# The opening of a two-block transformer kernel, reordered: weights of blocks 0 and 1 two chunks at a time, block 2 in halves, x on ScalarE's queue, first sum of squares behind block 5

## The chip, the cores and the metric

The kernel runs on one core of a Trainium2 chip. The metric is the device time of one execution in microseconds (us), the median of several runs. The profile is one execution recorded by the hardware profiler on the same kernel; its times are counted from the start of its span.

## What is computed

The reference is a stack of two transformer blocks on x of 256 tokens by 1024 features, all in float32:

```python
x = first_block(x, ...)    # ffn, mixer (indexed attention and pooling), ffn
return second_block(x, ...)  # ffn, gated mixer, ffn, final norm
...
x = x + 0.5 * swiglu(rms_norm(x, ffn1_norm[l]), ffn1_w_gate[l], ffn1_w_up[l], ffn1_w_down[l])
...
def rms_norm(x, g):
    xf = x.astype(jnp.float32)
    y = xf * lax.rsqrt(jnp.mean(xf * xf, axis=-1, keepdims=True) + NORM_EPS)
    return (y * g.astype(jnp.float32)).astype(x.dtype)
def swiglu(x, w_gate, w_up, w_down):
    return (jax.nn.silu(x @ w_gate) * (x @ w_up)) @ w_down
```

The change touches only the start of the first feed-forward stage (`ffn1`), with D = 1024 and 2816 hidden features.

## The kernel before

All weights of the program lie in HBM as one stream of blocks of 128 x 1024 floats (512 KB). A block of the gate or up matrix holds the weights of 128 hidden features for all eight chunks (k = 0 to 7) of 128 input features. Gate and up blocks alternate: block 2f is the gate and 2f + 1 the up of hidden chunk f. The stream passes through a ring of four slots (`RING`): SyncE (SP) issues the DMA of block n as soon as the low part of block n - 4 is made (semaphore `w_split`), ScalarE copies it to `w_hi`, rounded to the short float format of TensorE (`split`, L479), VectorE subtracts to get the remainder `w_lo` (`split`, L867), and TensorE multiplies. x is treated alike: `x_hi` on ScalarE (L486, times the norm's gain), `x_lo` on VectorE (L873), side by side in `x_hl`. TensorE makes two matmuls for each chunk of a block (`both`, L1396 and L1397): high weights times high and low x, 512 columns, then low weights times high x, 256 columns. Eight such pairs make a block (`wide_block`).

The norm is taken out of the matmul: the products are made with x unnormalised, and each result is scaled by `rstd`. Its chain in the first stage is: ScalarE squares the eight chunks of x (`square`, L482), POOL adds them up one after the other (`add_squares`, L382), TensorE sums over the partitions with a matmul by ones (`sum_squares`, L1464), VectorE makes the mean `ms` (L901), ScalarE the root (L520, which has a table load ahead of it), VectorE a reciprocal and three Newton steps (L894 to L897). Only then can VectorE scale the first hidden chunk (`add`: L936 adds the two halves of the products, L938 scales; `product`, L945). POOL issues the DMAs of the constants (L397 to L400) behind its adds.

Each engine runs its own program strictly in the order it is written by hand; the semaphores only make it wait. In `ffn` VectorE makes the low parts of blocks 3 to 6, then `mean_square`, then block 7, then `inverse_root`, then `add(0)`, block 8, `product(0)`, `add(1)`, block 9 and so on. ScalarE makes the high parts of blocks 3 to 7 and then the root.

The opening is written apart. SP loads blocks 0 and 1 in halves of 512 columns (chunks 0 to 3, then 4 to 7), then chunks 4 to 7 of x, then blocks 2 and 3 whole. ScalarE issues x chunks 0 and 1, the column gains `cols`, and x chunks 2 and 3. x comes in four pairs of chunks (`x_loaded`). TensorE first runs `WARM` = 16 matmuls on zeros. It then takes, for each chunk k of x, block 0 and block 1 (`for k ...: for c in range(2)`) into two banks, then blocks 2 and 3, the sum of squares, and blocks 4 and on. Block 7 needs bank 3, in which the sum of squares lies, and waits for `ms_done`:

```python
for f in range(2, LEAD):
    if f == 3:
        pe.wait_ge(ms_done, p + 1)
    elif f >= 4:
        pe.wait_ge(parts_added, FC * e + f - 3)
    chunk(f, (f + 2) % 4)
```

Of the kernel before, what the change touches and what calls it, by code (L numbers as in the profile page):

```python
# [26 lines left out]
P = 128  # L27
# [19 lines left out]
RING = 4  # L47
# [46 lines left out]
def build(nc, stream, x_in, cols_in, rows_in, const_in, sgu_w_in, pool_w_in, gain_in, out):  # L94
    ctx = ExitStack()
    with ctx:
# [110 lines left out]
        half_arrived = [sem(f"half_arrived{i}") for i in range(2)]  # L207
# [136 lines left out]
        def _(sp):  # L344
            for n in range(2):
                sp.dma_start(w_raw[:, n, 0:HALF], stream[n, :, 0:HALF]).then_inc(half_arrived[n], 16)
            for n in range(2):
                sp.dma_start(w_raw[:, n, HALF:BW], stream[n, :, HALF:BW]).then_inc(arrived[n], 16)
            for c in range(2, 4):
                sp.dma_start(x[:, 2 * c:2 * c + 2, :], x_in[:, 2 * c:2 * c + 2, :]).then_inc(x_loaded[c], 16)  # L350
            for n in range(2, RING):
                sp.dma_start(w_raw[:, n, :], stream[n]).then_inc(arrived[n], 16)
# [116 lines left out]
        def _(act):  # L469
# [18 lines left out]
            def first_input():  # L488

                for c in range(4):  # L490
# [3 lines left out]
                    if c == 1:  # L494
                        for n in range(2):
                            act.wait_ge(arrived[n], 16)
                            nc.scalar.activation(w_hi[:, n, HALF:BW], w_raw[:, n, HALF:BW], ACT.Copy).then_inc(w_hi_done, 1)
                    if 1 <= c < 3:
                        square(0, 2 * c - 2)
                        square(0, 2 * c - 1)  # L500
                split(2)
                for k in range(4, KC):
                    square(0, k)
# [18 lines left out]
            def ffn(e, n0, p):  # L522
                for b in range(3, 8):
# [307 lines left out]
            act.dma_start(x[:, 0:2, :], x_in[:, 0:2, :]).then_inc(x_loaded[0], 16)  # L831
            act.dma_start(cols[:, 0:NCOLS], cols_in).then_inc(cols_loaded, 16)
            act.dma_start(x[:, 2:4, :], x_in[:, 2:4, :]).then_inc(x_loaded[1], 16)
            act.wait_ge(filled, 1)
            nc.scalar.activation(spare[:], zeros[:, 0:1], ACT.Copy).then_inc(spare_set, 1)
            for n in range(2):
                act.wait_ge(half_arrived[n], 16)
                nc.scalar.activation(w_hi[:, n, 0:HALF], w_raw[:, n, 0:HALF], ACT.Copy).then_inc(half_hi_done, 1)
            act.wait_ge(cols_loaded, 16)
# [11 lines left out]
        def _(dve):  # L851
# [513 lines left out]
            for n in range(2):  # L1365
# [3 lines left out]
            for k in range(4):  # L1369
                input_lo(0, k)  # L1370
            for n in range(2):
# [3 lines left out]
            for k in range(4, KC):  # L1375
                input_lo(0, k)
            split(2)
# [9 lines left out]
        def _(pe):  # L1387
# [121 lines left out]
            def ffn(e, n0, p):  # L1509

                if p == 0:
                    pe.wait_ge(half_split, 2)
                for k in range(KC):
                    if k == (KC // 2 if p == 0 else 0):
                        pe.wait_ge(w_split, n0 + 2)
                    pe.wait_ge(x_split, 8 * p + k + 1)
                    w = slice(k * P, (k + 1) * P)
                    for c in range(2):
                        slot = (n0 + c) % RING
                        last = both(bank[4 + c][:, :], w_hi[:, slot, w], w_lo[:, slot, w], x_hl[:, k, :, :], k == 0, k == KC - 1)  # L1520
                        if k == KC - 1:
                            last.then_inc(w_used, 1)
                wide_block(n0 + 2, bank[6], x_hl)
# [279 lines left out]
WARM = 16  # L1803
# [112 lines left out]
```

## Time and profile before

| | |
|---|---|
| median of 3 runs | 1060.01 us (1059.9 to 1060.06) |
| the profiled execution's own time | 1060.34 us |
| its span | 1058.5 us |
| mean granted clock of TensorE | 0.999 |
| TensorE busy | 1048.3 us (99%) |
| VectorE busy | 773.9 us (73%) |
| ScalarE busy | 614.1 us (58%) |
| POOL busy | 193.0 us (18%) |
| moved by DMA | 200.53 MB, 189 GB/s on the mean |

The profile gives, for each engine, its instructions in order of time, each with its start, its length, and the idle time before it with the engine or transfer that ended it. ScalarE is called ACT there, VectorE DVE, TensorE PE, its weight loads PEld, and the queue part of an engine has a q (SPq, ACTq). The span is shorter than the execution's own time, which has some 1.8 us around it. The chain of work that ended last is 97% TensorE.

### The profile page before, as it was taken

To read this page: it belongs to the slowest core of one execution; us is meant where nothing else is said; L and a number is where in the kernel's file an instruction comes from. 1 tells how busy PE (TensorE), PEld (TensorE's weight loads), DVE (VectorE), ACT (ScalarE), POOL (GpSimd) and SP (SyncE) were. 2 spreads that over 40 slices of the span, in tenths; PEclk is the share of its full clock that TensorE was granted. 3 is DMA by queue.
4 is the path that set the end of the run, shared out by engine and by line. 5 is a ranking of instruction groups with operands and counts; after the bars stand their busy time and mean duration, and the time that the engine had idled before them with its cause. 6 is when DMAs were issued, how large, how long until landed. Compare 5 with 4: busy or idle time off the path is not lost.

```text
span 1058.5 us, 17547 instructions
## 1 busy us (share of the span) xinstructions
PE 1048.3 (99%) x6112; PEld 920.2 (87%) x6112; DVE 773.9 (73%) x1107; ACT 614.1 (58%) x936; POOL 193.0 (18%) x208
## 2 busy tenths in 40 slices
PE   8999999999999999999999999999999999999997
PEld 6888888888888888888888888889988888888886
DVE  6876776799797666668767666788877778877543
ACT  7655545466765654447565445755655556655542
POOL 4211131020221111101111100133201032311100
PEclk9999999999999999999999999999999999999999
DMA  7855555554266565566555564656555555655552
GB/s 276 290 192 198 190 188 183 175 180 161 98 210 207 190 190 186 191 196 200 198 189 191 180 206 151 224 182 193 176 195 182 185 179 192 224 196 197 176 188 75
DMA packets 55570, 200.53 MB, mean 189 GB/s; under 512 B 6304, under 2 KB 6304, under 8 KB 55392
## 3 DMA queue, kind: packets, MB, share of 16 engines
q1 hardware_dynamic: 54288, 195.85, 56.0%
q0 software_dynamic: 656, 3.18, 0.8%
q10 hardware_dynamic: 576, 0.83, 0.3%
q8 instruction: 32, 0.52, 0.2%
q14 instruction: 18, 0.15, 0.0%
HBM read 198.78 MB, written 1.05 MB: 189 GB/s over the span
## 4 chain that ended last, share of the span: by engine, by line
PE 97%; ACT 1%; DMA 1%; DVE 1%; issue 0%; ACTq 0%; DVEq 0%
PE pair L1396 52%; PE pair L1397 26%; PE pair L1390 6%; PE pair L1391 5%; PE pair L1392 5%; DMA x<-x_in 1%; PE pair L1743 0%; PE pair L1676 0%; PE pair L1663 0%; PE pair L1607 0%; PE pair L1654 0%; PE pair L1464 0%; ACT qk_a L698 0%; ACT x_hl L486 0%; DVE qk_a L1178 0%; PE pair L1640 0%
## 5 line engine op out<-in xcount | busy, mean ns | idle before, releaser
L867 DVE TENSOR_TENSOR w_lo<-w_raw,w_hi 128x1024 fp32r<-128x1024 f32 x369 | 461.6, 1255 | 213.5 <-ACT w_hi L479 212.8
L1396 PE MATMUL pair<-x_hl,w_hi 128*128 128x512 f32 x1728 | 591.5, 390 | 2.6 <-DVE x_hl L873 2.4
L479 ACT ACTIVATE w_hi<-w_raw 128x1024 fp32r<-128x1024 f32 x369 | 386.1, 1057 | 229.9 <-PE pair L1397 181.4
L1397 PE MATMUL pair<-x_hl,w_lo 128*128 128x256 f32 x1728 | 477.8, 277 | 0.0
L1396 PEld LDWEIGHTS pair<-x_hl,w_hi 128*128 128x128 f32 x1728 | 324.4, 188 | 71.0 <-issue 3.2
L1397 PEld LDWEIGHTS pair<-x_hl,w_lo 128*128 128x128 f32 x1728 | 324.3, 188 | 0.1
L1396 PE MATMUL pair<-wide,w_hi 128*128 128x512 f32 x720 | 247.2, 391 | 0.0
L1397 PE MATMUL pair<-wide,w_lo 128*128 128x256 f32 x720 | 199.6, 277 | 0.0
L1396 PEld LDWEIGHTS pair<-wide,w_hi 128*128 128x128 f32 x720 | 135.2, 188 | 28.8
L390 POOL TENSOR_TENSOR wide<-side,wide 128x256 fp32r<-128x256 f32 x88 | 86.6, 984 | 377.4 <-ACT wide L537 377.4
L1397 PEld LDWEIGHTS pair<-wide,w_lo 128*128 128x128 f32 x720 | 135.1, 188 | 0.0
L382 POOL TENSOR_TENSOR x_sq<-x_sq 128x256 f32<-128x256 f32 x42 | 40.4, 962 | 239.3 <-ACT x_sq L482 238.0
L486 ACT ACTIVATE x_hl<-x,cols 128x256 fp32r<-128x256 f32 x48 | 23.5, 507 | 78.0 <-DVE x L984 70.9
L936 DVE TENSOR_TENSOR tmp<-pair,side 128x512 f32<-128x512 f32 x88 | 60.3, 685 | 3.2 <-ACT side L529 2.8
L529 ACT ACTIVATE side<-pair 128x512 f32<-128x512 f32 x88 | 51.0, 580 | 5.2 <-PE pair L1397 5.2
L533 ACT ACTIVATE tmp<-tmp 128x256 f32<-128x256 f32 x88 | 35.9, 408 | 19.5 <-DVE tmp L938 19.5
L938 DVE TENSOR_TENSOR tmp<-tmp,rstd 128x256 f32<-128x256 f32 x88 | 44.2, 502 | 3.1
L1390 PE MATMUL pair<-w_hi,x_hl 128*128 128x512 f32 (+1 forms) x112 | 43.4, 387 | 0.0
L1391 PE MATMUL pair<-w_lo,x_hl 128*128 128x512 f32 (+1 forms) x112 | 42.4, 379 | 0.0
L1392 PE MATMUL pair<-w_hi,x_hl 128*128 128x512 f32 (+1 forms) x112 | 42.4, 379 | 0.0
L537 ACT ACTIVATE wide<-side 128x256 f32 (+1 forms) x88 | 35.9, 408 | 5.2 <-DVE side L945 5.2
L945 DVE TENSOR_TENSOR side<-tmp 128x256 f32<-128x256 f32 x88 | 36.8, 418 | 1.9 <-ACT tmp L533 1.9
(199 smaller groups left out, 860.5 us busy)
## 6 DMA issues: line engine op xcount, KB each, us to landing
w_raw<-stream SPq DMA_DIRECT2D x369, 512.0 KB, 3.3
const<-const_in POOLq DMA_DIRECT2D x1, 1248.0 KB, 8.3
w_raw<-stream SPq DMA_DIRECT2D x4, 256.0 KB, 5.6
rows<-rows_in POOLq DMA_DIRECT2D x1, 576.0 KB, 10.2
x<-x_in ACTq DMA_DIRECT2D x2, 256.0 KB, 5.6
x<-x_in SPq DMA_DIRECT2D x2, 256.0 KB, 6.6
sgu_w<-sgu_w_in POOLq DMA_DIRECT2D x1, 512.0 KB, 12.9
qk_a<-gain_in POOLq DMA_DIRECT2D x1, 512.0 KB, 4.0
```

The source lines that it names most:

```text
L382: nc.gpsimd.tensor_tensor(x_sq[:, 0, :], x_sq[:, 0, :], x_sq[:, k, :], ALU.add).then_inc(x_sq_added, 1)
L390: nc.gpsimd.tensor_tensor(hid_lo[:, f, :], hid_b[:, f % 2, :], hid_hi[:, f, :].bitcast(F32), ALU.subtract).then_inc(hid_split, 1)
L479: nc.scalar.activation(w_hi[:, slot, at:at + BW], w_raw[:, slot, :], ACT.Copy).then_inc(w_hi_done, 1)
L529: nc.scalar.activation(low_s[:], pair[j][:, :, S:2 * S], ACT.Copy).then_inc(low_copied, 1)
L867: nc.vector.tensor_tensor(w_lo[:, slot, :], w_raw[:, slot, :], w_hi[:, slot, at:at + BW].bitcast(F32), ALU.subtract).then_inc(w_split, 1)
L936: nc.vector.tensor_tensor(sum_s, pair[j][:, :, 0:S], low_s[:], ALU.add).then_inc(parts_added, 1)
L938: nc.vector.tensor_tensor(gate_s, gate_s, rstd[:], ALU.mult).then_inc(gate_scaled, 1)
L1390: nc.tensor.matmul(dst, a_hi, b_hi, start=first, stop=False, skip_group_check=True)
L1391: nc.tensor.matmul(dst, a_hi, b_lo, start=False, stop=False, skip_group_check=True)
L1392: return nc.tensor.matmul(dst, a_lo, b_hi, start=False, stop=last, skip_group_check=True)
L1396: nc.tensor.matmul(dst, a_hi, b_hl.rearrange("p a s -> p (a s)"), start=first, stop=False, skip_group_check=True)
L1397: return nc.tensor.matmul(dst[:, 0:S], a_lo, b_hl[:, 0, :], start=False, stop=last, skip_group_check=True)
```

## The change

SP issues the halves of blocks 0 and 1, then block 2 in halves, then block 3 whole; it issues no x any more. ScalarE issues `cols` first and then the four pairs of x. ScalarE and VectorE make their parts in the order half of block 0, pair 0 of x, half of block 1, pair 1, second half of block 0, pair 2, second half of block 1, pair 3, the halves of block 2. On ScalarE all squares but two come behind block 3. TensorE takes two chunks of block 0, the same two chunks of block 1, and so on, and then block 2, waiting for its halves. In the first stage the sum of squares stands behind block 5 instead of block 3, and the wait for `ms_done` stands between blocks 6 and 7. There are 15 matmuls on zeros instead of 16. The other stages keep their order.

```diff
@@ SP @@
-            for n in range(2):
+            def first_half(n):
                 sp.dma_start(w_raw[:, n, 0:HALF], stream[n, :, 0:HALF]).then_inc(half_arrived[n], 16)
-            for n in range(2):
+
+            def second_half(n):
                 sp.dma_start(w_raw[:, n, HALF:BW], stream[n, :, HALF:BW]).then_inc(arrived[n], 16)
-            for c in range(2, 4):
-                sp.dma_start(x[:, 2 * c:2 * c + 2, :], x_in[:, 2 * c:2 * c + 2, :]).then_inc(x_loaded[c], 16)
-            for n in range(2, RING):
-                sp.dma_start(w_raw[:, n, :], stream[n]).then_inc(arrived[n], 16)
+
+            first_half(0)
+            first_half(1)
+            second_half(0)
+            second_half(1)
+            first_half(2)
+            second_half(2)
+            sp.dma_start(w_raw[:, 3, :], stream[3]).then_inc(arrived[3], 16)
@@ ScalarE @@
+                first_half(0)
+                act.wait_ge(cols_loaded, 16)
+                x_pair(0)
+                first_half(1)
+                x_pair(1)
+                second_half(0)
+                x_pair(2)
+                second_half(1)
+                x_pair(3)
+                first_half(2)
+                second_half(2)
+                square(0, 0)
+                square(0, 1)
+                split(3)
+                for k in range(2, KC):
                     square(0, k)
...
-                for b in range(3, 8):
+                for b in range(4 if p == 0 else 3, 8):
                     split(n0 + b)
...
-            act.dma_start(x[:, 0:2, :], x_in[:, 0:2, :]).then_inc(x_loaded[0], 16)
             act.dma_start(cols[:, 0:NCOLS], cols_in).then_inc(cols_loaded, 16)
-            act.dma_start(x[:, 2:4, :], x_in[:, 2:4, :]).then_inc(x_loaded[1], 16)
+            for c in range(4):
+                act.dma_start(x[:, 2 * c:2 * c + 2, :], x_in[:, 2 * c:2 * c + 2, :]).then_inc(x_loaded[c], 16)
@@ VectorE @@
+            first_half(0)
+            input_lo(0, 0)
+            input_lo(0, 1)
+            first_half(1)
+            input_lo(0, 2)
+            input_lo(0, 3)
+            second_half(0)
+            input_lo(0, 4)
+            input_lo(0, 5)
+            second_half(1)
+            input_lo(0, 6)
+            input_lo(0, 7)
+            first_half(2)
+            second_half(2)
             ffn(0, START[0], 0)
@@ TensorE, ffn @@
+                def opening(k, c):
+                    slot, w = (n0 + c) % RING, slice(k * P, (k + 1) * P)
+                    if c == 0:
+                        pe.wait_ge(x_split, 8 * p + k + 1)
+                    last = both(bank[4 + c][:, :], w_hi[:, slot, w], w_lo[:, slot, w], x_hl[:, k, :, :], k == 0, k == KC - 1)
+                    if k == KC - 1:
+                        last.then_inc(w_used, 1)
+
                 if p == 0:
-                    pe.wait_ge(half_split, 2)
...
+                    for two in range(0, KC, 2):
+                        for c in range(2):
+                            if two < KC // 2:
+                                pe.wait_ge(half_split, c + 1)
+                            else:
+                                pe.wait_ge(w_split, c + 1)
+                            opening(two, c)
+                            opening(two + 1, c)
+                    pe.wait_ge(half_split, 3)
+                    for k in range(KC):
+                        if k == KC // 2:
+                            pe.wait_ge(w_split, 3)
+                        opening(k, 2)
...
                 wide_block(n0 + 3, bank[7], x_hl)
-                sum_squares(p)
+                if p:
+                    sum_squares(p)
 
                 def chunk(f, j, i=0):
 
                     wide_block(n0 + 2 * f, bank[2 * j], x_hl, i, 8)
+                    if p == 0 and f == 3:
+                        pe.wait_ge(ms_done, p + 1)
                     wide_block(n0 + 2 * f + 1, bank[2 * j + 1], x_hl, i, 8)
 
                 for f in range(2, LEAD):
-                    if f == 3:
+                    if f == 3 and p == 0:
+                        sum_squares(p)
+                    elif f == 3:
                         pe.wait_ge(ms_done, p + 1)
...
-WARM = 16
+WARM = 15
```

ScalarE's program before, from its first DMA to the high part of block 3 (L486 is a high part of x, L838 and L497 halves of blocks 0 and 1, L482 squares):

```order
L831 DMA x<-x_in 128x512
L832 DMA cols<-cols_in 128x84
L833 DMA x<-x_in 128x512
...
L838 ACTIVATE w_hi<-w_raw 128x512 [waits half_arrived0]
L838 ACTIVATE w_hi<-w_raw 128x512 [waits half_arrived1]
L486 ACTIVATE x_hl<-x,cols 128x256 [waits x_loaded0,cols_loaded]
...
L482 ACTIVATE x_sq<-x 128x256 x4
L479 ACTIVATE w_hi<-w_raw 128x1024 [waits arrived3]
L479 ACTIVATE w_hi<-w_raw 128x1024 [waits w_used,arrived0]
```

The same place in the changed program:

```order
L851 DMA cols<-cols_in 128x84
L853 DMA x<-x_in 128x512 x4
...
L497 ACTIVATE w_hi<-w_raw 128x512 [waits half_arrived0]
L491 ACTIVATE x_hl<-x,cols 128x256 [waits x_loaded0,cols_loaded]
L491 ACTIVATE x_hl<-x,cols 128x256
L497 ACTIVATE w_hi<-w_raw 128x512 [waits half_arrived1]
...
L487 ACTIVATE x_sq<-x 128x256 x2
L484 ACTIVATE w_hi<-w_raw 128x1024 [waits arrived3]
L487 ACTIVATE x_sq<-x 128x256 x6
L484 ACTIVATE w_hi<-w_raw 128x1024 [waits w_used,arrived0]
```

Pair 0 of x has moved ahead of the half of block 1 and behind the gains in the queue, and six squares now stand between blocks 3 and 4.

TensorE around the sum of squares before (pair0 to pair3 are the bank pairs; each block is 16 rows of matmuls, the rows of its other chunks are left out):

```order
L1397 MATMUL pair3<-x_hl,w_lo 128x256
L1464 MATMUL pair1<-x_sq,ones 128x256 [waits x_sq_added]
L1396 MATMUL pair0<-x_hl,w_hi 128x512 [waits w_split]
...
L1396 MATMUL pair1<-x_hl,w_hi 128x512 [waits w_split,ms_done]
```

and in the changed program:

```order
L1424 MATMUL pair0<-x_hl,w_lo 128x256
L1491 MATMUL pair1<-x_sq,ones 128x256 [waits x_sq_added]
L1423 MATMUL pair1<-x_hl,w_hi 128x512 [waits w_split]
...
L1423 MATMUL pair1<-x_hl,w_hi 128x512 [waits w_split,ms_done]
```

The matmul by ones has moved from ahead of block 4 (pair0) to ahead of block 6 (pair1), and the wait for the mean from block 6 to block 7. VectorE's program behind it has kept its order, which reads in the changed program (L883 is a block's low part, L952 and L954 the addition and scaling of a hidden chunk):

```order
L883 TENSOR_TENSOR w_lo<-w_raw,w_hi 128x1024 [waits w_hi_done] x4
L917 TENSOR_SCALAR ms<-pair 128x256 [waits sumsq_done]
L883 TENSOR_TENSOR w_lo<-w_raw,w_hi 128x1024 [waits w_hi_done]
L910 RECIPROCAL rstd<-root 128x256 [waits root_done]
...
L952 TENSOR_TENSOR tmp<-pair,side 128x512 [waits low_copied,rstd_done]
L954 TENSOR_TENSOR tmp<-tmp,rstd 128x256 [waits parts_added]
L883 TENSOR_TENSOR w_lo<-w_raw,w_hi 128x1024 [waits w_hi_done]
```

Of this, only the count ahead of `ms` differs (x4, block 2 having its own halves; before x5).

## Rows read from the trace of the kernel before

**Rows 1.** The page, part 1: busy time, share of the span, instructions

```profile
PE 1048.3 (99%) x6112; PEld 920.2 (87%) x6112; DVE 773.9 (73%) x1107; ACT 614.1 (58%) x936; POOL 193.0 (18%) x208
```

**Rows 2.** Timeline of PE, 0 to 46 us: start, length, engine, line, operation, idle before

```profile
1.33 5.19 PE L1788 MATMUL pair<-zeros 128*128 128x512 bf16 x16 [1.33 <-POOL zeros L372]
8.16 0.47 PE L1396 MATMUL pair<-x_hl,w_hi 128*128 128x512 f32 x1 [1.64 <-DVE x_hl L873]
...
11.97 0.47 PE L1396 MATMUL pair<-x_hl,w_hi 128*128 128x512 f32 x1 [0.78 <-DVE x_hl L873]
...
15.22 0.50 PE L1396 MATMUL pair<-x_hl,w_hi 128*128 128x512 f32 x1 [0.22 <-DVE w_lo L867]
...
20.93 0.59 PE L1464 MATMUL pair<-x_sq,ones 128*128 128x256 f32 x2
...
21.70 0.39 PE L1396 MATMUL pair<-x_hl,w_hi 128*128 128x512 f32 x1
...
24.43 0.39 PE L1396 MATMUL pair<-x_hl,w_hi 128*128 128x512 f32 x1
```

**Rows 3.** Timeline of DVE, 0 to 60 us

```profile
6.07 0.69 DVE L1367 TENSOR_TENSOR w_lo<-w_raw,w_hi 128x512 fp32r<-128x512 f32 x1 [6.07 <-ACT w_hi L838]
...
7.53 0.88 DVE L873 SCALAR_TENSOR_TENSOR x_hl<-x,cols,x_hl 128x256 fp32r<-128x256 f32 x2
...
16.11 6.12 DVE L867 TENSOR_TENSOR w_lo<-w_raw,w_hi 128x1024 fp32r<-128x1024 f32 x4 [0.95 <-ACT w_hi L479]
22.16 0.41 DVE L901 TENSOR_SCALAR ms<-pair 128x256 f32<-128x256 f32 x1
22.49 1.21 DVE L867 TENSOR_TENSOR w_lo<-w_raw,w_hi 128x1024 fp32r<-128x1024 f32 x1
24.01 1.75 DVE L894 RECIPROCAL rstd<-root 128x256 f32<-128x256 f32 x1 [0.31 <-ACT root L520]
...
28.24 1.22 DVE L867 TENSOR_TENSOR w_lo<-w_raw,w_hi 128x1024 fp32r<-128x1024 f32 x1
...
31.28 1.21 DVE L867 TENSOR_TENSOR w_lo<-w_raw,w_hi 128x1024 fp32r<-128x1024 f32 x1
...
34.31 1.21 DVE L867 TENSOR_TENSOR w_lo<-w_raw,w_hi 128x1024 fp32r<-128x1024 f32 x1
```

**Rows 4.** Timeline of ACT, 0 to 60 us

```profile
5.40 0.63 ACT L838 ACTIVATE w_hi<-w_raw 128x512 fp32r<-128x512 f32 x1 [1.74 <-DMA w_raw<-stream]
6.26 0.63 ACT L838 ACTIVATE w_hi<-w_raw 128x512 fp32r<-128x512 f32 x1 [0.22 <-DMA w_raw<-stream]
6.79 0.89 ACT L486 ACTIVATE x_hl<-x,cols 128x256 fp32r<-128x256 f32 x2
8.17 0.91 ACT L486 ACTIVATE x_hl<-x,cols 128x256 fp32r<-128x256 f32 x2 [0.48 <-DMA x<-x_in]
...
13.80 1.33 ACT L482 ACTIVATE x_sq<-x 128x256 f32<-128x256 f32 x4
15.03 2.95 ACT L479 ACTIVATE w_hi<-w_raw 128x1024 fp32r<-128x1024 f32 x3
...
22.27 1.28 ACT L520 ACT_TABLE_LOAD   x1
23.56 0.42 ACT L520 ACTIVATE root<-ms 128x256 f32<-128x256 f32 x1
```

**Rows 5.** SP's issues of x (timeline), and the time to landing at line L350

```profile
2.61 1.43 SPq L350 DMA_DIRECT2D x<-x_in  x2
...
DMA to landing us min/median/max: 6.6/6.6/6.6
```

**Rows 6.** Timeline of POOL, 0 to 60 us

```profile
14.29 5.73 POOL L382 TENSOR_TENSOR x_sq<-x_sq 128x256 f32<-128x256 f32 x4 [0.59 <-ACT x_sq L482]
```

**Rows 7.** The same sum of squares in the last feed-forward stage, timeline 880.5 to 882 us

```profile
881.00 0.59 PE L1464 MATMUL pair<-x_sq,ones 128*128 128x256 f32 x2
...
881.63 0.42 DVE L901 TENSOR_SCALAR ms<-pair 128x256 f32<-128x256 f32 x1 [0.85 <-PE pair L1464]
```

More of the change, by code:

```diff
@@ L206, in build @@
         arrived = [sem(f"arrived{i}") for i in range(RING)]
-        half_arrived = [sem(f"half_arrived{i}") for i in range(2)]
+        half_arrived = [sem(f"half_arrived{i}") for i in range(3)]
         half_hi_done = sem("half_hi_done")
@@ L488, in first_input, with first_half, second_half, x_pair @@
             def first_input():
-                for c in range(4):
+                def first_half(n):
+                    act.wait_ge(half_arrived[n], 16)
+                    nc.scalar.activation(w_hi[:, n, 0:HALF], w_raw[:, n, 0:HALF], ACT.Copy).then_inc(half_hi_done, 1)
+                def second_half(n):
+                    act.wait_ge(arrived[n], 16)
+                    nc.scalar.activation(w_hi[:, n, HALF:BW], w_raw[:, n, HALF:BW], ACT.Copy).then_inc(w_hi_done, 1)
+                def x_pair(c):
                     act.wait_ge(x_loaded[c], 16)
@@ L493, in first_input @@
                     input_hi(0, 2 * c + 1)
[L494 to L502, printed above, removed]
+                first_half(0)
[13 more added lines that the diff above has]
+                for k in range(2, KC):
                     square(0, k)
@@ L829, in gated_mixer @@
                     square(p + 1, m)
-            act.dma_start(x[:, 0:2, :], x_in[:, 0:2, :]).then_inc(x_loaded[0], 16)
             act.dma_start(cols[:, 0:NCOLS], cols_in).then_inc(cols_loaded, 16)
-            act.dma_start(x[:, 2:4, :], x_in[:, 2:4, :]).then_inc(x_loaded[1], 16)
+            for c in range(4):
+                act.dma_start(x[:, 2 * c:2 * c + 2, :], x_in[:, 2 * c:2 * c + 2, :]).then_inc(x_loaded[c], 16)
             act.wait_ge(filled, 1)
             nc.scalar.activation(spare[:], zeros[:, 0:1], ACT.Copy).then_inc(spare_set, 1)
[L836 to L839, printed above, removed]
             first_input()
@@ L1363, in gated_mixer, with first_half @@
                 input_lo(p + 1, KC - 1)
-            for n in range(2):
+            def first_half(n):
                 dve.wait_ge(half_hi_done, n + 1)
@@ L1368, in _, with second_half @@
                                         ALU.subtract).then_inc(half_split, 1)
-            for k in range(4):
-                input_lo(0, k)
-            for n in range(2):
+            def second_half(n):
                 dve.wait_ge(w_hi_done, n + 1)
@@ L1374, in _ @@
                                         ALU.subtract).then_inc(w_split, 1)
-            for k in range(4, KC):
-                input_lo(0, k)
-            split(2)
+            first_half(0)
[12 more added lines that the diff above has]
+            second_half(2)
             ffn(0, START[0], 0)
@@ L1509, in ffn @@
             def ffn(e, n0, p):
-                if p == 0:
-                    pe.wait_ge(half_split, 2)
[L1513 to L1522, printed above, removed]
@@ L1523, in ffn @@
-                wide_block(n0 + 2, bank[6], x_hl)
+                def opening(k, c):
[5 more added lines that the diff above has]
+                        last.then_inc(w_used, 1)
+                if p == 0:
+                    for two in range(0, KC, 2):
[11 more added lines that the diff above has]
+                        opening(k, 2)
+                else:
+                    pe.wait_ge(w_split, n0 + 2)
+                    for k in range(KC):
+                        for c in range(2):
+                            opening(k, c)
+                    wide_block(n0 + 2, bank[6], x_hl)
```

## The prediction, made before the changed kernel was run

> **What bounds the kernel now.** I began with the busy time of the page: TensorE is busy for 1048.3 of 1058.5 us [rows 1], so only some 10 us of the span can be won without giving TensorE less to do, and the change gives it one warm matmul less and nothing else. Next I read TensorE's own timeline for where these 10 us lie. From 1.33 to 6.52 it runs 16 matmuls on zeros; the first real one starts at 8.16; it stops before 11.97 and before 15.22, both times with an idle time written at the row [rows 2]. From there on the pairs of matmuls (512 columns, then 256) follow each other every 0.34 to 0.35 us: two rows that are eight pairs apart stand at 21.70 and 24.43, so that a block costs 2.73 us [rows 2]. I found no TensorE wait between this and the end of the kernel. So the opening is the only stretch from which the change can take time, and everywhere behind it the question is by how much each producer leads TensorE. For that I read the timelines of ScalarE (high parts of weights and x, squares), VectorE (low parts) and POOL (adding squares).
>
> **The opening.** Its ends before: a low half of a block costs VectorE 0.69 us, from 6.07 to 6.76, and two low parts of x take 0.88 us from 7.53 on, the first of them until about 8.0; TensorE starts at 8.16, some 0.15 us later [rows 3, 2]. ScalarE needs 0.53 us from one weight half to the next operation (6.26 to 6.79), 0.40 for a high part of x (0.89 for a pair with the tail of the last), 0.33 for a square and about 0.98 for a whole block [rows 4]. It got pair 1 of x at 8.14 to 8.17, after 0.48 us of waiting for the transfer [rows 4].
>
> With the new order I take ScalarE through its queue. Half of block 0 ends at 6.04, as now (VectorE's row at 6.07 waited for it). Pair 0 of x can then start if it is there; the column gains now go ahead of it on the same queue, so I take its landing at 6.3, which is an estimate: the bytes before it (half of blocks 0 and 1, pair 0, gains) are those that had landed when ScalarE began pair 0 at 6.79 [rows 4]. Then: pair 0 6.3, half of block 1 7.1, pair 1 8.15 (it still waits for its transfer), second half of block 0 8.95, pair 2 9.5, second half of block 1 10.3, pair 3 10.8, block 2 in halves 11.6 and 12.1, squares 0 and 1 12.7, block 3 13.3, the other six squares 14.2, block 4 16.1, block 5 17.1. For pairs 2 and 3 I need landings by 9.5 and 10.8. On the SP queue they were issued from 2.61 on and landed 6.6 us after issue, at 9.2 and 9.9 [rows 5]; now block halves are interleaved with them, and by their place in the sum of the bytes they land at about 9.2 and 10.5, just before they are wanted.
>
> A rule is weighed here: the rows give no sign that a transfer on the other queue would be faster (pair 1, issued by ScalarE, took until 8.14 while the halves were coming on SP). The Trainium skill, page "DMA: Bandwidth & Descriptors", section "Issuing engines are not separate DMA queues", says that transfers from all issuing engines run on the same 16 DMA engines and interleave, and that only issue time is saved. By it my landings stand; were the queues independent, pair 1 could start at 7.65 and TensorE could gain up to 0.5 us more.
>
> VectorE follows ScalarE closely: low half of block 0 6.76, low parts 0 and 1 of x 7.35 and 7.75, half of block 1 8.5, parts 2 and 3 9.2 and 9.6, second half of block 0 10.3, parts 4 and 5 10.7 and 11.1, second half of block 1 11.7, parts 6 and 7 12.1 and 12.5, block 2 13.1 and 13.7. TensorE, 0.35 us a pair of matmuls: 7.5 (two chunks of block 0), 8.65 (block 1), 9.35 to 10.75 (chunks 2 and 3), 10.85 and 11.85 (4 and 5), 12.55 to 13.95 (6 and 7). Block 2 starts at 13.95 and has no wait left, instead of 15.22. **Term one: -1.3 us.** Bounds: 0 if x lands late; at best TensorE starts at 7.5 and never stops, 16 x 0.35 = 5.6 us, block 2 at 13.1, so -2.1.
>
> Edits that cost nothing: the five DMA issues of ScalarE take about 0.45 us each and end near 3.0, the table load of 1.28 us and the spare operation then end near 4.6, before the first half arrives at 5.40 [rows 4] (ScalarE waited for it for 1.74 us; if that cover of 0.8 us went, the opening would move by the rest). One warm matmul fewer ends that stretch about 0.2 us sooner; TensorE stood idle from 6.52 to 8.16 before without a lower granted clock, so a gap from 6.3 to 7.5 is harmless. Block 2 in two halves costs each engine a tenth of a microsecond of start-up, inside the times above.
>
> Blocks 3 and 4 come later on ScalarE, because squares 2 to 7 stand between them: block 4 ends at 17.15 there. VectorE's four blocks from 16.11 took 6.12 us, 1.53 each, beside POOL's adds, whereas one beside nothing took 1.21 [rows 3]. I take 1.7 for block 4: ready at 18.9, wanted at 13.95 + 5.6 = 19.55. It holds, by 0.6 us. The Trainium skill, page "SBUF — State Buffer", section "Who interferes with whom", has VectorE operations with two SBUF inputs and GpSimd take one port pair by turns, each blocked for the whole of the other's instruction. By the mean of the rows (1.53) block 4 has 0.8 us to spare, by a full add of 1.43 us (5.73/4) in its way it would miss by 0.25, and the sum would be that much higher.
>
> **The sum of squares.** POOL's adds took 5.73 us for four [rows 6], 1.43 each; six of them from 15.0 end at 23.6. TensorE reaches the place behind block 5 at T = 13.95 + 16 x 0.35 + 2 x 2.73 = 25.0. So the matmul itself does not wait, and its own 0.43 us is only moved.
>
> What hangs on it does matter. Before, it started at 20.93 and block 6 followed two blocks later. The chain was: ms on VectorE, block 7's low part, root on ScalarE, reciprocal 24.01, three steps, the first block's addition and scaling, then the low part of **block 8** 28.24 to 29.46, blocks 9 and 10 from 31.28 and 34.31 (1.21 each, to 32.49 and 35.52) [rows 3]. In that order VectorE can't touch block 8 before the reciprocal and its Newton steps are through. TensorE wanted block 8 at 21.36 + 4 x 2.73 = 32.3 (21.36 is a pair before the row at 21.70), blocks 9 and 10 at 35.0 and 37.7: leads of 2.8, 2.5 and 2.2 us. The change takes two blocks, 5.46 us, out of that lead. What the chain gets back: ms came 1.23 us after the matmul because VectorE was busy with block 6 [rows 2, 3]; in the last feed-forward stage it came after 0.63 [rows 7], so 0.6. The root's table load of 1.28 us ran until 23.55 [rows 4] and was behind block 7's high part; now both are long done, so the reciprocal starts when block 7's low part ends, 0.63 + 0.33 + 1.24 = 2.2 us after T instead of 3.08. That is 0.88 in all. From the reciprocal on the durations are the same ones, VectorE being busy without a gap.
>
> So block 8 is ready at T + 7.65 and wanted at T + 0.43 + 5.46 = T + 5.9; block 9 at T + 10.7 against T + 8.6; block 10 at T + 13.7 against T + 11.35; block 11 is 1.5 us later than 10 and no longer late. The total of the stall is the largest lateness, 2.35 us, plus some 0.1 for restarting. **Term two: +2.5 us.** Bounds: 1.9 if ms and root cost 0.6 less than I think, 3.1 if the table load has to follow ms after all (0.63 + 0.42 + 1.28 + 0.42 = 2.75 in place of 2.2); 0 only if the order on VectorE isn't what binds. The stall can't be caught up later, since TensorE has no other idle time.
>
> **Sum:** -1.3 + 2.5 = +1.2 us. The profiled execution took 1060.34 us, which becomes 1061.5; it lies 0.33 above the median of the runs (1060.01), and from the median I get **1061.2 us**. A measurement of this kernel can tell about 0.2% (2.1 us) from no change, so this is "the same".
>
> **Rivals.**
> A. The opening gains and the lead holds, because ScalarE or VectorE gets block 8 done earlier than I read: -1.3, 1058.7 us. For it: the change moves the wait for ms with it, as if its place had been weighed. Against it: the fixed order on VectorE. With a gain at its bound of 2.1 it would touch 0.2% faster.
> B. Slower: pair 0 of x, now behind the gains and in ScalarE's queue ahead of half of block 1, lands late. ScalarE takes its work strictly in order, so everything behind it shifts. From a landing at about 7.5 us (1.2 later than I take) term one is gone, and +2.5 gives 1062.5 us, over 0.2%. For it: there are five DMAs on one queue. Against it: the same bytes had landed by 6.8 before.
> C. The x transfers do come faster than the byte count says, and term one is -1.8 to -2.1 with the stall kept: +0.6, 1060.6 us, the same.
>
> **How the numbers follow.** Forecast (opening gains about 1.3, stall of about 2.5) 0.62; A 0.14; B 0.13; C 0.11. Faster by over 0.2% needs A at its bound: 0.04. Slower by over 0.2% is B, or the forecast with its stall at the upper end: 0.14. The rest, 0.82, is within 0.2%. The range goes from A with 0.2 us more gained, 1058.5, to B with 0.4 more of stall, 1062.9.
>
> **What would show it.** Right: block 2 on TensorE near 14.0; the matmul of the sum of squares near 25; TensorE idle 1.5 to 2 us before block 8 (near 31) and a few tenths before blocks 9 and 10, released by VectorE's low part; reciprocal 2.2 us behind the matmul. Wrong: no idle time near 31 to 38 (then A), a ScalarE wait of over 1 us for x before 8 (then B), or an idle time before block 4.

## The result, and the profile after

The changed kernel takes 1062.67 us in the median of 8 runs (1061.62 to 1064.41), the kernel before 1060.02 in the same rounds (8 runs, 1059.86 to 1060.06). The ratio is 1.0028 with a 95% interval of 1.0019 to 1.0037: slower by 2.65 us, where 1.2 had been forecast and up to 2.1 had been called the same. The kernel before hardly varies; this one does. Five runs lie from 1061.62 to 1062.82 with a mean granted clock of 0.998 or 0.999, three from 1064.16 to 1064.41 with 0.997.

The profiled execution is the shortest of the eight, 1061.62 us, with a span of 1059.8. Against the profiled execution before it is 1.28 us longer. TensorE's timeline in it (start, length, engine, line, operation, idle before):

```profile
1.33 5.42 PE L1835 MATMUL pair<-zeros 128*128 128x512 bf16 x15 [1.33 <-POOL zeros L377]
6.85 0.47 PE L1423 MATMUL pair<-x_hl,w_hi 128*128 128x512 f32 x1
...
9.70 0.48 PE L1423 MATMUL pair<-x_hl,w_hi 128*128 128x512 f32 x1 [0.84 <-DVE x_hl L889]
...
14.29 0.39 PE L1423 MATMUL pair<-x_hl,w_hi 128*128 128x512 f32 x1
...
25.18 0.59 PE L1491 MATMUL pair<-x_sq,ones 128*128 128x256 f32 x2
...
32.87 0.47 PE L1423 MATMUL pair<-x_hl,w_hi 128*128 128x512 f32 x1 [1.64 <-DVE w_lo L883]
...
35.80 0.50 PE L1423 MATMUL pair<-x_hl,w_hi 128*128 128x512 f32 x1
...
38.92 0.47 PE L1423 MATMUL pair<-x_hl,w_hi 128*128 128x512 f32 x1
```

These answer to [rows 2]. The real matmuls start at 6.85 instead of 8.16, wait for pair 1 of x until 9.70, and reach block 2 at 14.29 instead of 15.22. The sum of squares is at 25.18. Before block 8, at 32.87, stands a stop of 1.8 us; blocks 9 (35.80) and 10 (38.92) start with short ones. VectorE behind it, as in [rows 3]:

```profile
17.51 4.59 DVE L883 TENSOR_TENSOR w_lo<-w_raw,w_hi 128x1024 fp32r<-128x1024 f32 x3 [1.57 <-ACT w_hi L484]
25.81 0.42 DVE L917 TENSOR_SCALAR ms<-pair 128x256 f32<-128x256 f32 x1 [3.70 <-PE pair L1491]
26.15 1.21 DVE L883 TENSOR_TENSOR w_lo<-w_raw,w_hi 128x1024 fp32r<-128x1024 f32 x1
27.28 1.74 DVE L910 RECIPROCAL rstd<-root 128x256 f32<-128x256 f32 x1
...
31.50 1.22 DVE L883 TENSOR_TENSOR w_lo<-w_raw,w_hi 128x1024 fp32r<-128x1024 f32 x1
...
34.53 1.21 DVE L883 TENSOR_TENSOR w_lo<-w_raw,w_hi 128x1024 fp32r<-128x1024 f32 x1
...
37.56 1.21 DVE L883 TENSOR_TENSOR w_lo<-w_raw,w_hi 128x1024 fp32r<-128x1024 f32 x1
```

The matmul by ones at T = 25.18 is answered at T + 0.63 by the mean, at T + 2.1 by the reciprocal, and the low parts of blocks 8, 9 and 10 end at T + 7.54, 10.56 and 13.59 (31.50 + 1.22 and so on). VectorE had waited 3.70 us for the mean with nothing to do. ScalarE and POOL, as in [rows 4, 6]:

```profile
5.67 0.91 ACT L491 ACTIVATE x_hl<-x,cols 128x256 fp32r<-128x256 f32 x2 [0.43 <-DMA x<-x_in]
...
8.53 0.91 ACT L491 ACTIVATE x_hl<-x,cols 128x256 fp32r<-128x256 f32 x2 [1.43 <-DMA x<-x_in]
...
14.59 1.94 ACT L487 ACTIVATE x_sq<-x 128x256 f32<-128x256 f32 x6
...
21.70 1.28 ACT L540 ACT_TABLE_LOAD   x1
26.27 0.42 ACT L540 ACTIVATE root<-ms 128x256 f32<-128x256 f32 x1 [3.28 <-DVE ms L917]
```

```profile
15.07 8.52 POOL L387 TENSOR_TENSOR x_sq<-x_sq 128x256 f32<-128x256 f32 x6 [0.40 <-ACT x_sq L487]
```

The table load is over long before the mean, so the root follows it at once. Pair 1 of x came to ScalarE at 8.53 (8.17 before), after a wait of 1.43 us. Block 4, which the prediction had ready at 18.9 us, was ready at about 19.0 (the first of the three subtractions from 17.51, 1.53 us each) and wanted at 19.7; no stop stands there.

### The profile page after: what moved, and what is told of

The parts are those of the page before. It is cut to its first block, busy times and chain, and to the rows that moved or that the text cites. A ratio compares the mean times of both kernels' runs of the same rounds, so it can differ in the third digit from the quotient of the medians.

```text
span 1059.8 us, 17550 instructions
## 1 busy us (share of the span) xinstructions
PE 1049.5 (99%) x6111; PEld 919.1 (87%) x6111; DVE 772.4 (73%) x1108; ACT 613.3 (58%) x937; POOL 193.9 (18%) x208
## 3 DMA queue, kind: packets, MB, share of 16 engines
q10 hardware_dynamic: 864, 1.35, 0.4%
HBM read 198.78 MB, written 1.05 MB: 189 GB/s over the span
## 4 chain that ended last, share of the span: by engine, by line
PE 97%; DVE 1%; DMA 1%; ACT 0%; issue 0%; ACTq 0%; DVEq 0%
PE pair L1423 52%; PE pair L1424 26%; PE pair L1417 6%; PE pair L1418 5%; PE pair L1419 5%; DMA x<-x_in 1%; PE pair L1790 0%; PE pair L1723 0%; PE pair L1710 0%; PE pair L1654 0%; PE pair L1491 0%; PE pair L1701 0%; ACT qk_a L718 0%; DVE w_lo L883 0%; DVE qk_a L1194 0%; PE pair L1687 0%
## 5 line engine op out<-in xcount | busy, mean ns | idle before, releaser
L883 DVE TENSOR_TENSOR w_lo<-w_raw,w_hi 128x1024 fp32r<-128x1024 f32 x368 | 459.9, 1254 | 213.4 <-ACT w_hi L484 213.2
L952 DVE TENSOR_TENSOR tmp<-pair,side 128x512 f32<-128x512 f32 x88 | 60.2, 684 | 3.2 <-ACT side L549 2.8
L954 DVE TENSOR_TENSOR tmp<-tmp,rstd 128x256 f32<-128x256 f32 x88 | 44.1, 502 | 3.1
```

The lines of the kernel that those rows point to most:

```text
L883: nc.vector.tensor_tensor(w_lo[:, slot, :], w_raw[:, slot, :], w_hi[:, slot, at:at + BW].bitcast(F32), ALU.subtract).then_inc(w_split, 1)
L952: nc.vector.tensor_tensor(sum_s, pair[j][:, :, 0:S], low_s[:], ALU.add).then_inc(parts_added, 1)
L954: nc.vector.tensor_tensor(gate_s, gate_s, rstd[:], ALU.mult).then_inc(gate_scaled, 1)
```

## The experiments

The profiled execution is what the sum had said. The others are longer, so two theories stood at first on what makes the runs spread from one execution to the next. W: the gaps in the opening let TensorE's clock fall. S: the stop before block 8 does. Later a third thing showed, the pace of the matmuls after a stop (P).

**e1, the changed kernel again.** No edit.

> The changed kernel once more. Its trace (1061.62 us) shows a stall before block 8 and otherwise TensorE at full clock, +1.3 us against the kernel before, as the sum had it; but its other runs reach 1064.4 with a mean granted clock of 0.997 instead of 0.999. Theory W (opening): in some executions TensorE runs part of the opening at the lower clock, because its first real matmuls now come with gaps in between, one of about 1 us before 9.70. Theory S (stall): the stall of 1.8 us before block 8 lets the clock fall in some executions. Both expect times spread from 1061.6 to 1064.4; a trace of one of the longer ones shows the rows at the lower clock before 15 us by W, behind 31 us by S.

1062.64 us in the median of 9 runs: seven from 1061.88 to 1062.80, one at 1066.67 (clock 0.999), one at 1068.69 (0.997). The trace (1062.47 us) is at full clock but 0.85 us longer than the first one, and all of that is there at block 2 already: pair 1 of x comes at 9.37, block 2 starts at 15.13. So besides the clock there are two more sources of spread: pair 1, and something worth 4 us that leaves the mean clock alone.

**e2, the kernel before with the sum of squares behind block 5.**

```diff
                 wide_block(n0 + 3, bank[7], x_hl)
-                sum_squares(p)
+                if p:
+                    sum_squares(p)
...
                     wide_block(n0 + 2 * f, bank[2 * j], x_hl, i, 8)
+                    if p == 0 and f == 3:
+                        pe.wait_ge(ms_done, p + 1)
...
-                    if f == 3:
+                    if f == 3 and p == 0:
+                        sum_squares(p)
+                    elif f == 3:
                         pe.wait_ge(ms_done, p + 1)
```

> The kernel before with one edit: in the first stage the sum of squares stands behind block 5 and the wait for the mean before block 7; opening, x and warm matmuls as before. Stall term by the prediction: +2.5 us, so 1062.5, with VectorE's low part of block 8 released about 7.65 us after the matmul by ones and TensorE idle about 1.8 us before block 8. By W all runs lie within 0.2 us of each other, since the opening is the old one. By S they spread upwards by 2 to 3 us as the changed kernel's do.

Two groups with nothing between: six runs from 1062.31 to 1062.65, five from 1066.85 to 1067.01, both at 0.998 to 1.000. The lower one is 2.45 us above the kernel before (1059.96), the stall term of the sum. TensorE and then VectorE in its trace, which is of the lower group:

```profile
26.05 0.59 PE L1464 MATMUL pair<-x_sq,ones 128*128 128x256 f32 x2
...
33.75 0.47 PE L1396 MATMUL pair<-x_hl,w_hi 128*128 128x512 f32 x1 [1.64 <-DVE w_lo L867]
```

```profile
26.68 0.42 DVE L901 TENSOR_SCALAR ms<-pair 128x256 f32<-128x256 f32 x1 [4.65 <-PE pair L1464]
...
28.16 1.75 DVE L894 RECIPROCAL rstd<-root 128x256 f32<-128x256 f32 x1
...
32.38 1.22 DVE L867 TENSOR_TENSOR w_lo<-w_raw,w_hi 128x1024 fp32r<-128x1024 f32 x1
```

Block 8 is ready 7.55 us after the matmul by ones, here as in the changed kernel, whatever the opening does. No run has a low clock although the stop before block 8 is there: S falls. The upper group came as a surprise to both theories.

**e3, 20 matmuls on zeros.** `WARM = 20` in the changed kernel.

> The changed kernel with 20 matmuls on zeros instead of 15 and nothing else. TensorE waits from 8.7 to 9.7 for x anyway, so five more warm matmuls at the full clock (1.07 us) cost nothing at the end. By W the runs close up near 1061.6, since the clock has risen before the real matmuls with their gaps begin; by S they stay spread up to 1064.

1063.13 us, 1061.92 to 1068.25. The runs did not close up as was expected by W; by the times alone S looked better. So W was wrong in that more warm-up would help, and only the trace tells the two apart. It is of the longest execution, 1068.25 us. The opening in stretches of 5 us (busy time of each engine, then granted clock, DMA share, GB/s), and TensorE's timeline in the middle one:

```profile
5.00:10.00 5.00, 3.77 (x19) 2.12 (x17) 2.27 (x4) 2.12 (x6) 0.00 (x0) 1.00 0.90 287
10.00:15.00 5.00, 4.33 (x16) 3.75 (x17) 4.93 (x10) 5.00 (x13) 0.23 (x1) 0.66 0.85 301
15.00:20.00 5.00, 5.00 (x31) 4.45 (x30) 2.80 (x4) 4.41 (x10) 4.33 (x4) 1.00 0.83 265
```

```profile
10.67 0.47 PE L1423 MATMUL pair<-x_hl,w_hi 128*128 128x512 f32 x1 [1.90 <-DVE x_hl L889]
...
11.67 0.63 PE L1423 MATMUL pair<-x_hl,w_hi 128*128 128x512 f32 x1
...
12.31 0.63 PE L1423 MATMUL pair<-x_hl,w_hi 128*128 128x512 f32 x1
```

Pair 1 came at 9.49, TensorE had stood still for 1.90 us, and just after it took up work the clock went from 2.4 to 1.2 GHz until 14.5: the pairs at 11.67 and 12.31 are 0.64 us apart, not 0.34, and block 2 starts at 16.45. This is W in the records: the fall is in the opening, and at the stop before block 8 (35.03 here) the clock stays up. The 3.4 us at half clock cost 1.7. The rest of the loss is elsewhere. The same two matmuls near 100 us, in e3 and then in e1:

```profile
99.61 0.39 PE L1423 MATMUL pair<-x_hl,w_hi 128*128 128x512 f32 x1
...
99.96 0.40 PE L1423 MATMUL pair<-x_hl,w_hi 128*128 128x512 f32 x1
```

```profile
99.67 0.39 PE L1423 MATMUL pair<-x_hl,w_hi 128*128 128x512 f32 x1
...
100.01 0.39 PE L1423 MATMUL pair<-x_hl,w_hi 128*128 128x512 f32 x1
```

0.35 against 0.34 us, at full clock and with no wait. From block 11 to the end of the first stage each pair of matmuls in e3 stands 350 ns behind the last, in e1 340. That is some 4.4 us of the 5.8 between the two spans, and as much as lies between the two groups of e2.

**e4, block 8 before the mean.** In the changed kernel's first stage ScalarE makes the high part of block 8 before the root, VectorE the low parts of 7 and 8 before the mean, and the later ones up to 13 each stand one place earlier:

```diff
+                ahead = 1 if p == 0 else 0
-                for b in range(3, 7):
+                for b in range(3, 9 if ahead else 7):
                     split(n0 + b)
                 mean_square(p)
-                split(n0 + 7)
+                if not ahead:
+                    split(n0 + 7)
                 inverse_root(p)
...
-                split(n0 + 8)
+                split(n0 + 8 + ahead)
```

> The changed kernel, but in the first stage ScalarE and VectorE make block 8 (and VectorE block 7) ahead of the mean square and the root, while they wait for the sum of squares anyway, and each later low part up to block 13 one place earlier. By the prediction's stall term the idle time before block 8 goes: 2.5 us less than the changed kernel, 1059.1 where that one has 1061.6. If the stall had another cause (the ring's transfers or the addition that frees the bank) it stays. By S the spread goes with the stall, by W it stays.

1060.28 us, 1059.81 to 1061.56, 2.4 below the changed kernel beside it; none of 11 runs is above 1062. TensorE at block 8:

```profile
32.43 0.50 PE L1428 MATMUL pair<-x_hl,w_hi 128*128 128x512 f32 x1 [0.21 <-DVE tmp L956]
```

The stop shrinks from 1.8 to some 0.2 us and is now ended by the addition that frees the bank (L956), not by a low part. The median is 1.2 above the 1059.1 expected, for two reasons. Block 8's weights landed late (ScalarE waited 2.81 us for them until 25.38), which pushed the mean back by 0.8 us: against e1's trace, which reaches block 2 at nearly the same time (15.13, here 15.28), 2.0 us are won and not 2.5. And the 1059.1 was reckoned from the first trace, with pair 1 at 8.53; here it came at 9.51. Three runs are at a clock of 0.997, 1061.13 to 1061.56: the spread by the clock stays without the stop. S falls here too.

**e5, a matmul by ones between blocks 10 and 11 of the changed kernel.** The matmul is the one of the sum of squares and goes to a bank that the next block begins anew:

```diff
+                    if p == 0 and f == 5:
+                        nc.tensor.matmul(bank[2 * j + 1][:, 0:S], ones[:], x_sq[:, 0, :], start=True, stop=True,
+                                         skip_group_check=True)
```

> The changed kernel with one more matmul by ones (the same one as the sum of squares, 0.43 us) between blocks 10 and 11, where the stalls have ended. Traces so far: in one execution of 1068.25 us the pairs of matmuls follow each other every 350 ns from block 11 to the end of the first stage instead of 340 (some 450 pairs, 4.5 us); in the kernel before they do so every 350 ns from the stop before block 2 until the sum of squares and every 340 after it. Theory P (pace): after a stall TensorE can settle at 350 ns and a different matmul lets it fall back to 340. Then no run is above 1065.5 us; the rest lies 0.4 above the changed kernel, 1062.2 to 1064.8. If the pace has another cause, runs at 1066.5 to 1068.7 stay, 2 to 5 in 11.

1063.58 us, 1062.90 to 1064.74; only 5 runs, none in the upper group. With about one in four expected there this says little alone, so e9 repeats it on e2's kernel.

**e6, the wait filled.** Eight matmuls on zeros between the first two chunks of block 1 and the wait for pair 1 of x.

> The changed kernel with eight matmuls on zeros between the first two chunks of block 1 and the wait for pair 1 of x, so that TensorE isn't idle there. Theory W: the clock falls in some executions because of this wait (in a trace of e3 it fell to the lower level at 11.1 us for 3.4 us, after 1.9 us of waiting for pair 1). Then no run shows a mean clock of 0.997 with its 1.5 to 1.7 us, and the low group is at 1061.9 to 1062.8, at most 0.6 later where pair 1 comes early. The pace at 350 ns stays possible, so some runs at 1066 to 1067 may stay. Were the stall before block 8 the cause of the clock's fall, 0.997 stays in 1 to 4 runs of 11.

1062.89 us; seven runs from 1062.60 to 1063.34, all at 0.998 to 1.000, and one at 1067.35 with 0.999. None has the low clock, and one stands in the upper group, as expected of the stop that is left. In the trace pair 1 comes at 9.41 and the clock stays up.

**e7, x issued as before.** The changed kernel, but ScalarE issues pair 0, the gains and pair 1, and SP pairs 2 and 3 behind the second halves of blocks 0 and 1.

> The changed kernel with x issued as before: pair 0, gains, pair 1 by ScalarE, pairs 2 and 3 by SP behind the second halves of blocks 0 and 1, block 2's halves behind them. If moving x to ScalarE's queue is what makes pair 1 late (8.5 to 9.5 us in the traces of the changed kernel, 8.0 to 8.2 before), pair 1 is there at 8.2 at the latest, block 2 starts at 14.0 as forecast, and the fast runs fall to 1061.2, close together and without a mean clock of 0.997. If the order of the weight halves does it, pair 1 stays at 8.5 to 9.5 and the times stay.

1061.32 us: ten runs from 1060.94 to 1061.58, two at 1065.53 and 1065.82, none at a low clock. ScalarE and TensorE in the trace:

```profile
8.34 0.91 ACT L493 ACTIVATE x_hl<-x,cols 128x256 fp32r<-128x256 f32 x2 [0.63 <-DMA x<-x_in]
```

```profile
14.11 0.39 PE L1425 MATMUL pair<-x_hl,w_hi 128*128 128x512 f32 x1
```

Pair 1 is there at 8.34 (8.2 had been expected), block 2 starts at 14.11, and the lower group, 1061.3 in its median, stands where the forecast for the whole change stood, 1061.2. Undoing one part, how x and the gains are issued, takes 1.35 us off the median, and no run has the low clock. What the transfers do differently shows from 4 to 8 us (columns as in e3's table, GB/s last), in the kernel before, the changed kernel and e7:

```profile
4.00:8.00 4.00, 2.51 (x11) 0.84 (x9) 1.77 (x4) 2.06 (x4) 0.00 (x0) 1.00 1.01 345
4.00:8.00 4.00, 3.81 (x15) 1.59 (x14) 2.27 (x4) 2.66 (x6) 0.00 (x0) 1.00 0.82 256
4.00:8.00 4.00, 3.75 (x13) 1.51 (x12) 1.84 (x4) 2.06 (x4) 0.00 (x0) 1.00 0.99 338
```

The changed kernel moves a quarter less in this stretch, and e1, e3, e4, e5 and e6 are lower still, 218 to 237 GB/s.

**e8, a version against the late pair, the stall and the spread.** The changed opening with the pairs of x in SP's queue in the order of use, squares in the pauses, and the sum of squares behind block 4:

```diff
             first_half(0)
             first_half(1)
+            sp.dma_start(x[:, 2:4, :], x_in[:, 2:4, :]).then_inc(x_loaded[1], 16)
             second_half(0)
+            sp.dma_start(x[:, 4:6, :], x_in[:, 4:6, :]).then_inc(x_loaded[2], 16)
             second_half(1)
+            sp.dma_start(x[:, 6:8, :], x_in[:, 6:8, :]).then_inc(x_loaded[3], 16)
             first_half(2)
...
                 first_half(1)
+                square(0, 0)
+                square(0, 1)
                 x_pair(1)
...
                     wide_block(n0 + 2 * f, bank[2 * j], x_hl, i, 8)
+                    if p == 0 and f == 2:
+                        sum_squares(p)
```

> A version to beat both. The changed opening, but pairs 1 to 3 of x stand in SP's queue between the weight halves in the order of use (ScalarE issues gains and pair 0 only), ScalarE squares two chunks in each pause so that POOL is done earlier, and the sum of squares stands behind block 4 instead of 5. By the prediction's sums: pair 1 at about 7.6, block 2 at 13.2 (-2.0), the chain's lead is one block more than in the changed kernel, so block 10 is ready 0.4 us ahead of TensorE and no stall is left: 1058.0 us, all runs close together. If the stall term isn't what I hold it to be, or POOL is late with its adds, 1059 to 1061.

1058.69 us in the median of 11 runs (1058.04 to 1059.05) beside 1059.99: ratio 0.9988, interval 0.9979 to 0.9997. It beats both kernels; the median is 0.7 above the 1058.0 expected, the lowest run at it. TensorE, ScalarE, POOL and VectorE in its trace (1058.04 us):

```profile
6.60 0.47 PE L1429 MATMUL pair<-x_hl,w_hi 128*128 128x512 f32 x1 [0.56 <-DVE x_hl L895]
...
13.18 0.39 PE L1429 MATMUL pair<-x_hl,w_hi 128*128 128x512 f32 x1
...
21.36 0.59 PE L1497 MATMUL pair<-x_sq,ones 128*128 128x256 f32 x2
...
35.41 0.39 PE L1429 MATMUL pair<-x_hl,w_hi 128*128 128x512 f32 x1
```

```profile
7.37 0.90 ACT L494 ACTIVATE x_hl<-x,cols 128x256 fp32r<-128x256 f32 x2
```

```profile
11.29 8.41 POOL L390 TENSOR_TENSOR x_sq<-x_sq 128x256 f32<-128x256 f32 x6 [3.01 <-ACT x_sq L490]
```

```profile
27.69 1.22 DVE L889 TENSOR_TENSOR w_lo<-w_raw,w_hi 128x1024 fp32r<-128x1024 f32 x1
...
33.74 1.21 DVE L889 TENSOR_TENSOR w_lo<-w_raw,w_hi 128x1024 fp32r<-128x1024 f32 x1
```

Pair 1 needs no wait at 7.37, block 2 starts at 13.18, POOL is done at 19.7, and block 10 is ready at 34.95, T + 13.59 as in the changed kernel. TensorE begins it at 35.41, straight behind block 9: the lead is back, 0.46 us of it. No idle time is written behind the first real matmul's; the short stops between the pairs up to block 2 add up to some 1.1 us (6.58 us for 16 pairs of 0.34). The new places of x, of the squares and of the sum were not tried one by one.

**e9, e2's kernel with the matmul by ones between blocks 10 and 11; e10, e2's kernel again; e11, e8's kernel again.** The edits are those of e5, none, and none.

> The kernel of e2 (before, sum of squares behind block 5) with one more matmul by ones between blocks 10 and 11. In e2 six runs stood at 1062.3 to 1062.65 and five at 1066.85 to 1067.01, with nothing between. Theory P: the upper group is the pace of 350 ns per pair, kept from the last stop (before block 10) to the end of the first stage, and a different matmul ends it. Then all runs are at 1062.7 to 1063.1 and none at 1067.3. If the pace has nothing to do with what follows the stop, about four or five runs in 11 stand near 1067.3.

> The kernel of e2 once more, beside e9 on the same chip. By P two groups again, 1062.4 and 1066.9, with 2 to 6 of 11 in the upper one; if the profiled execution falls in the upper group its matmul pairs stand 350 ns apart from block 11 to the end of the first stage. If there is no upper group here, e9 says nothing about P.

> The kernel of e8 once more. If e8's gain is the kernel's and not of that chip or hour, 1058.0 to 1059.1 again, the median near 1058.6, none at 1062 or above (no stall behind block 8, so nothing that the pace of 350 ns could follow).

e9: 1063.16 us, all 7 runs between 1062.78 and 1063.36, a little above what was expected and no upper group. e10: eight runs from 1062.25 to 1062.65 and two at 1066.75 and 1067.17. e11: 1058.62 us, 1058.07 to 1059.11. e9's trace happens to hold the slow pace at the end of block 10 and what the added matmul does to it:

```profile
41.87 0.40 PE L1396 MATMUL pair<-x_hl,w_hi 128*128 128x512 f32 x1
...
42.22 0.40 PE L1396 MATMUL pair<-x_hl,w_hi 128*128 128x512 f32 x1
...
42.92 0.59 PE L1534 MATMUL pair<-x_sq,ones 128*128 128x256 f32 x2
43.16 0.58 PE L1396 MATMUL pair<-x_hl,w_hi 128*128 128x512 f32 x1
```

Up to 42.92 the pairs are 0.35 us apart (41.87, 42.22), and from 43.70 on they are 0.34 apart. The other traces say the same of the sum of squares itself: in those of the kernel before, e6, e9 and e11 the pairs of blocks 2 and 3 and on to the sum of squares stand 350 ns apart and behind it 340, and in no trace does 350 go on behind a matmul by ones (one or two pairs behind it are still at 350).

The counts of runs say less. Over all runs of kernels with the stop and no matmul by ones behind it 16 of 69 are in the upper group; with the matmul it is 0 of 12, which at that rate would be chance once in 24 times. e9 and e10, side by side, have 0 of 7 and 2 of 10. Where no such stop stands behind the last matmul by ones, in the kernel before, e8 and e11, it is 0 of 110, and in e4 with its 0.2 us 0 of 11. P stands, by the traces more than by the counts. Two things stay open: only one trace, e3's, is of an execution of the upper group, so that the others keep the slow pace to the end of the stage is taken from their extra 4.5 us; and no run put a short pause there without a matmul. What inside TensorE differs between the two paces no run here shows.

## Why the prediction was wrong

**The stall: right.** Term two said that block 8 is ready at T + 7.65, that the largest lateness is block 10's, and +2.5 us. The first trace has T + 7.54 and a total of 2.49 (the end is 1.29 us later although the place behind block 5 is reached 1.20 earlier), and e2, the stall alone, has +2.45 in its lower group. Rival A, that the lead holds, fell with it: it is the fixed order of the producers that binds. e4 changes only this order, on VectorE and with it on ScalarE, and the stop goes from 1.8 to 0.2 us.

**The opening: the arithmetic right, one input wrong.** The step that failed is "pair 1 8.15 (it still waits for its transfer)". I let pair 1 land as before because the bytes ahead of it were the same. In the six traces with x on ScalarE's queue ScalarE got it at 8.53 in the changed kernel's first and at 9.35 to 9.51 in e1, e3, e4, e5 and e6; with the old issues at 7.95 to 8.34 (before, e2, e7, e9, e10); with the pairs among the halves on SP's queue at 7.37 and 7.44 (e8, e11). So term one is -1.2 at best, as in the first trace, and about -0.3 in the usual one: e1 reaches block 2 at 15.13 against 15.22. What stands behind pair 1 in ScalarE's order kept the lengths of the sum. Half of block 0 arrived earlier than I had taken it: ScalarE began it without a wait at 4.64 (5.40 before), and at 3.81 in e8, both with the small transfer of the gains ahead of pair 0; with pair 0 ahead, in e7, at 5.39. So TensorE started at 6.85 and not at 7.5, but that time is only spent waiting for pair 1.

Taking the landing from the bytes ahead failed in two ways. The rate was lower, 256 GB/s from 4 to 8 us against 345. This alone makes pair 1 late in the first trace: 1.88 MB had been moved when it came, 1.83 in the kernel before and 1.89 in e7. And in e1, e3 and e4 more had been moved when it came, 2.09 to 2.15 MB, so other transfers had gone ahead of it. The Trainium skill, page "DMA: Bandwidth & Descriptors", section "Issuing engines are not separate DMA queues", says that all transfers run on the same 16 DMA engines and that issuing from several engines saves issue time only. Here the queue changed more than that, the rate and the landing both. Why the rate falls no run shows; it is as low in e8 (265 GB/s), where pair 1 is early all the same because it stands early in its queue.

Rival B was this mechanism with the wrong pair. It had pair 0 late, and 1062.5 us; pair 0 came at 5.67, earlier than before, and pair 1 was the one that came late.

**The clock: missed altogether.** The sentence that "a gap from 6.3 to 7.5 is harmless" was about the gap before the first real matmul. The gap that matters comes behind the first four pairs, where TensorE waits for pair 1. In 11 of 44 runs of kernels with x on ScalarE's queue and nothing in this wait (the changed kernel, e1, e3, e4, e5) the mean clock is 0.997 or less; with the wait filled (e6) or the transfers as before (e7) it is none of 20. In the one trace that shows the fall, e3's, it is worth 1.7 us. The mean tells it only roughly: behind the last matmuls every trace has a stretch at 1.2 GHz (0.62 granted from 1055 us to the end before), by which the mean varies between 0.998 and 1.000 anyway, so a run at 0.998 can hide a fall. The kernel before has a stop of 1.64 us at 8.16 and never shows 0.997 in 88 runs, and e4 and e5 have waits for pair 1 of 1.74 and 1.56 us in traces at full clock, so it isn't the length of one gap alone. What else it takes stays open.

**The pace: not in the sum.** The prediction took 2.73 us for a block from the trace before and had no term for a slower one. In runs of its upper group it costs 4.4 us.

**The forecast's size.** The profiled execution, 1061.62 us, is at the 1061.5 that the sum gave for it, and that is luck in part: it is the one trace of six in which pair 1 came near its forecast. Even there block 2 starts 0.9 us earlier and not 1.3; the other 0.3 of the -1.2 is the slow pace that the trace before has from block 2 to the sum of squares and this one has not. The median is 1.05 above it. The four other runs at full clock lie 0.2 to 1.2 us above, as a later pair 1 would give (0.85 us in e1's trace; these four have none), and the three at the low clock 2.5 to 2.8. The measured median is still inside the range given, near its upper end of 1062.9, but that end was meant for a late pair 0 with a longer stall. What I took to be one number was a spread with the sum at its lower edge.

## What to carry to other kernels

Before an operation that releases a long chain is moved back, count the lead of the work that stands behind this chain on the same engine: here two blocks, 5.46 us, out of a lead of 2.2 with 0.9 given back. When a transfer moves to another queue, don't reckon its landing from the sum of the bytes; measure it in several executions. Here the order of use within one queue brought pair 1 by 7.4 us, and four pairs in a queue of their own at 8.5 to 9.5. Look at more than one trace: the first one here was the best case. A short stop of TensorE can cost more than its length: here 2.5 us in most runs, and 4.5 more in about one of four.

## What the runs showed of the hardware that I had not expected

The same pair of matmuls can follow each other every 340 or every 350 ns at full clock without any wait. In the traces the pace changes only where TensorE takes up work after a stop or passes a different matmul (the first two or three pairs behind it apart); in e3 it is kept for over 150 us (4.4 us in all). The trace of the kernel before has it too, in blocks 2 and 3 behind the stop before block 2, where the sum of squares ends it; e2 and e10, with the same opening, have 340 there. Nothing told me that this matmul did such a service. Moved ahead of the stop, as by this change, it no longer can. In e11 the slow pace in the opening makes the sum of squares 0.3 us later than in e8 (21.65, 21.36).

TensorE's clock fell to 1.2 GHz for 3.4 us after 1.90 us of waiting in e3, though it had run at 2.4 GHz before and a few matmuls had just been made; the same kind of wait in e1, e5 and e4 (1.32, 1.56 and 1.74 us idle) left it alone.

With the four pairs of x on ScalarE's queue the transfers moved 218 to 256 GB/s from 4 to 8 us in six traces; in the five with the old issues it was 338 to 365.
